# Routing of a two-layer streaming encoder on one core: the router's logits moved between the projection's products, and the first expert's tokens gathered by 10 wide products instead of 40 narrow ones

## The reference, cut to what matters

```python
def _moe(x, router_w, router_b, w_gate, w_up, w_down):
    xt = x.reshape(-1, D)
    logits = xt.astype(F32) @ router_w.astype(F32) + router_b.astype(F32)
    probs = jax.nn.softmax(logits, axis=-1)
    ...                      # best group, then top_p, top_i inside it -> combine
    for e in range(N_EXPERTS):
        h = jax.nn.silu(xt @ w_gate[e]) * (xt @ w_up[e])
        y = y + combine[:, e:e + 1] * (h @ w_down[e]).astype(F32)

# in each layer, after the mixer:
yp = _post_norm(yp, mp, ln_mix_g[l], ln_mix_b[l])
yp = _post_norm(yp, _moe(yp, router_w, router_b, moe_w_gate[l], moe_w_up[l], moe_w_down[l]), ln_ffn_g[l], ln_ffn_b[l])
```

## Time and profile before

| | |
|---|---|
| Median of three runs | 1509.43 us (1508.6 to 1513.21) |
| Profiled execution, own time | 1504.01 us |
| its span, first to last instruction | 1502.1 us |
| mean granted TensorE clock, share of full speed | 0.878 |
| PE busy | 1242.7 us (83%) |
| DVE busy | 1019.8 us (68%) |
| ACT busy | 701.2 us (47%) |

### The profile page before, as it was taken

The page is one execution under the profiler, slowest core; times in us unless marked ns, Lnnn a source line. Parts: engine busy times, 40 slices in busy tenths (PEclk is TensorE's granted clock), DMA queues, the critical chain, the costliest instruction groups (busy, mean ns, idle before and its releaser), DMA issues.

```text
span 1502.1 us, 17364 instructions
## 1 busy us (share of the span) xinstructions
PE 1242.7 (83%) x6836; PEld 995.0 (66%) x6836; DVE 1019.8 (68%) x1039; ACT 701.2 (47%) x623; POOL 199.3 (13%) x219
## 2 busy tenths in 40 slices
PE   6998998797889999996594362989978899999960
PEld 5898888585767766664473362967867676677740
DVE  5883656445468878786857998342464688888848
ACT  4642322104177777675123243541251777777730
POOL 2020000000400000001102972000004000000021
PEclk9998988697699999998796685999976999999985
DMA  9456010333589999997453008350135899999955
GB/s 271 192 60 115 5 60 6 83 127 112 192 319 391 385 378 385 371 379 272 104 83 72 0 3 64 113 198 13 45 112 193 318 380 379 376 388 387 388 163 154
DMA packets 79279, 301.79 MB, mean 201 GB/s; under 512 B 23156, under 2 KB 40912, under 8 KB 66864
## 3 DMA queue, kind: packets, MB, share of 16 engines
q1 hardware_dynamic: 63128, 246.07, 48.0%
q0 software_dynamic: 16096, 54.96, 11.7%
HBM read 265.01 MB, written 33.64 MB: 199 GB/s over the span
## 4 chain that ended last, share of the span: by engine, by line
PE 57%; DVE 20%; DMA 12%; ACT 5%; issue 4%; SPq 2%; POOL 0%; DVEq 0%; ACTq 0%; POOLq 0%
PE ps L2300 15%; PE ps L2302 14%; PE ps L2301 14%; DMA raw<-in_moe_w_down 7%; DVE wlo L695 4%; ACT whi L611 3%; PE ps L762 3%; DMA u_d<-ub 2%; PE ps L1706 2%; PE ps L378 2%; DVE s_jtmp L1508 1%; DMA raw<-in_w_in_ab 1%; PE ps L2410 1%; DVE s_wt L1465 1%; PE ps L1704 1%
## 5 line engine op out<-in xcount | busy, mean ns | idle before, releaser
L695 DVE TENSOR_TENSOR wlo<-raw,whi 128x4096 fp32r<-128x4096 f32 x92 | 406.6, 4421 | 124.8 <-ACT whi L611 124.8
L611 ACT ACTIVATE whi<-raw 128x4096 fp32r<-128x4096 f32 x92 | 333.7, 3629 | 121.2 <-DMA raw<-in_moe_w_down 108.1
L2300 PE MATMUL ps<-whi,xet_lo 128*96 128x512 f32 x528 | 213.5, 404 | 18.1 <-issue 13.6
L2302 PE MATMUL ps<-whi,xet_hi 128*96 128x512 f32 x528 | 210.6, 399 | 0.0
L2301 PE MATMUL ps<-wlo,xet_hi 128*96 128x512 f32 x528 | 210.3, 398 | 0.0
L2300 PEld LDWEIGHTS ps<-whi,xet_lo 128*96 128x96 f32 x528 | 88.0, 167 | 62.5 <-issue 28.7
L2300 PE MATMUL ps<-ft_hi,wlo 128*128 128x288 f32 x384 | 120.7, 314 | 5.9 <-DVE wlo L2047 3.4
L2301 PE MATMUL ps<-ft_lo,whi 128*128 128x288 f32 x384 | 117.7, 307 | 0.0
L2302 PE MATMUL ps<-ft_hi,whi 128*128 128x288 f32 x384 | 117.6, 306 | 0.0
L2302 PEld LDWEIGHTS ps<-whi,xet_hi 128*96 128x96 f32 x528 | 86.6, 164 | 37.5 <-issue 0.5
L2301 PEld LDWEIGHTS ps<-wlo,xet_hi 128*96 128x96 f32 x528 | 86.9, 165 | 33.5 <-issue 0.5
(11 more groups left out here) (453 smaller groups left out, 2225.5 us busy)
## 6 DMA issues: line engine op xcount, KB each, us to landing
raw<-in_moe_w_gate SPq DMA_DIRECT2D x32, 2048.0 KB, 9.9
raw<-in_moe_w_up SPq DMA_DIRECT2D x32, 2048.0 KB, 9.6
raw<-in_moe_w_down SPq DMA_DIRECT2D x32, 2048.0 KB, 10.1
yg<-ysb POOLq DMA_DIRECT2D x32, 384.0 KB, 6.0
xe<-xg POOLq DMA_DIRECT2D x30, 384.0 KB, 9.0
raw<-in_w_in_ab SPq DMA_DIRECT2D x16, 512.0 KB, 7.5
raw<-in_w_out_s SPq DMA_DIRECT2D x4, 2048.0 KB, 8.5
xg<-zeros POOLq DMA_DIRECT2D x4, 1536.0 KB, 14.8
```

Source lines behind the costliest of these rows:

```text
L611: sa.activation(whi[q][:], raw[q][:], ACT.Copy).then_inc(s(f"hi{q}" + L), 1)
L695: v.tensor_tensor(wlo[q][:], raw[q][:], whi[q][:].bitcast(F32), ALU.subtract).then_inc(s(f"lo{q}" + L), 1)
L2300: te.matmul(out, l_lo, r_hi, start=first, stop=False)
L2302: return te.matmul(out, l_hi, r_hi, start=False, stop=last)
```

## The change

It has three parts, each in both layers.

- The router's steps are issued one tile earlier or more. `route_between` puts a transpose (and once logits) between the two halves of a tile's projection, and `route_early` puts logits behind the tile. Only the last tile's transpose and logits stay in `route_pe`. ACT's copies and square roots are put in the matching order.
- `xt_first` holds `onehot` as the weights and moves `xtok` in rows of 512: 2 halves x 5 tiles, 10 products, into banks 2 and 3. The result is token-major, so ACT copies it half by half into `xe`, and PE transposes it with the 8 transposes that the other experts use (`x_turned`).
- `keep_warm` issues products whose result is not used (bank 2): four after the last logits, two after the counting products.

```diff
         def route_early(pe, l, i):
-            if i >= 3:
-                logits(pe, l, i - 3)
+            if i == 1:
+                x1_transpose(pe, l, 0)
             if i >= 2:
-                x1_transpose(pe, l, i - 2)
+                logits(pe, l, i - 1)
+
+        def route_between(pe, l, i):
+            if i == 2:
+                logits(pe, l, 0)
+            if i >= 2:
+                x1_transpose(pe, l, i - 1)
+
+        def keep_warm(x, n, bank, times):
+            for _ in range(times):
+                nc.tensor.matmul(ps[0:n, bank, :], ident[0:n, 0:n], x, start=True, stop=True)
 
         def route_pe(pe, l):
             te = nc.tensor
-            logits(pe, l, NT - 3)
-            x1_transpose(pe, l, NT - 2)
-            logits(pe, l, NT - 2)
             x1_transpose(pe, l, NT - 1)
             logits(pe, l, NT - 1)
+            keep_warm(xtok[0:TT, 0, 0:512], TT, 2, 4)
             pe.wait_ge(s("chosen"), 2 * l + 1)
...
                       ).then_inc(s("ranked"), 1)
+            keep_warm(xtok[0:TT, 0, 0:512], TT, 2, 2)
...
             hi(2, 0, "")
+            for half in range(2):
+                act.wait_ge(s("ranked"), 3 * l + 2 + half)
+                sa.activation(xe[0:CAP, 512 * half:512 * half + 512], ps[0:CAP, 2 + half, :], ACT.Copy).then_inc(s("r_exp"), 1)
             xt_hi(0)
...
                 pe.wait_ge(s("chosen"), 2 * l + 2)
-                for k in range(KT):
+                for half in range(2):
                     for i, (t0, n) in enumerate(TILES):
-                        ins = te.matmul(ps[:, 4 + k // 4, P * (k % 4):P * (k % 4) + CAP], xtok[0:n, i, k:D:KT],
-                                        onehot[0:n, i, :], start=(i == 0), stop=(i == NT - 1))
-                ins.then_inc(s("p_xt" + L), 1)
+                        ins = te.matmul(ps[0:CAP, 2 + half, :], onehot[0:n, i, :], xtok[0:n, i, 512 * half:512 * half + 512],
+                                        start=(i == 0), stop=(i == NT - 1))
+                    ins.then_inc(s("ranked"), 1)
+                pe.wait_ge(s("r_exp"), 3 * l + 3)
+                x_turned()
...
                     act.wait_ge(s("y"), 2 * NT + j + 1)
...
-                    if ph and i:
-                        ln_act(act, "mix1", [i - 1])
-                    if ph and i >= 2:
-                        x1t_copy(act, 1, i - 2)
+                    if ph and i == 1:
+                        x1t_copy(act, 1, 0)
+                    if ph:
+                        ln_act(act, "mix1", [i])
...
             for i in range(NT):
+                if i:
+                    x1t_copy(act, 0, i - 1)
                 ln_act(act, "mix0", [i])
-                if i >= 2:
-                    x1t_copy(act, 0, i - 2)
-            x1t_copy(act, 0, NT - 2)
             route_act(act, 0)
```

## The result

| | before | after |
|---|---|---|
| Median of 20 runs each, us | 1510.08 (1504.32 to 1515.80) | 1523.05 (1512.11 to 1533.23) |
| Ratio, 95% interval | | 1.0082 (1.0064 to 1.0099) |
| Profiled execution, own time | 1504.01 | 1522.25 |
| Span | 1502.1 | 1520.5 |
| Mean granted clock | 0.878 | 0.892 |

The change made the kernel slower by 0.8%; forecast was no change. The runs of one kernel differ by up to 21 us, and the medians of the kernel before by 8.6 from chip to chip (1501.5 to 1510.1). So the experiments are compared by their ratio to runs of the kernel before on the same chip. A profile shows one execution of them.

The account below looks back on a forecast made before the run. Two paths of some 30 us, over PE and over POOL and transfers, end together at the second expert's tokens. Terms -1.6 - 0.6 + 1.8 = -0.4 us gave 1503.6 profiled, 1509.0 on the median; range 1503 to 1515.

Parts of the forecast that it names:

- Logits inside the projection: Router: last product ends 4.9 us later, yet logits are read 2.0 us earlier in layer 0, 1.0 in layer 1.
- Ten wide products: Expert 0's gather: 8.65 us at full clock for 19.5; expert 0's first product 10.5 and 9.5 us earlier.
- The next wait: After expert 0's products, PE waits some 8 us for the second expert's tokens, where it did not wait before.
- I take the middle: Second expert's token load, layer 0: landing taken as 412.2, between 410.2 (undisturbed) and 414.1 (behind the third gate load).
- S: The second expert's first product, at 417.57 in layer 0; forecast at 415.95, 1.6 us earlier, and 0.6 earlier in layer 1.
- Rival 3: Second expert's token load waits for the whole 8.8 us gate load; +5.9 us, 1515.3; chance 0.12.
- Rival 1: Second expert's token load is not held up by the gate load; -4.4 us, 1505.0; chance 0.16.
- The clock at S: Products at S start at half clock after PE's wait; 0.9 us per layer counted against the gain.
- What moves S moves the end: Loop behind S: PE is nearly always busy (19.94 of 20 us), so a shift of S shifts the end.

Follow-up runs that it names:

- before_act: The kernel before with two one-column copies and two waits more on ACT in each layer, results unused; ratio 1.0041 (1.0018 to 1.0064).
- hold: The changed kernel, with the third gate matrix's load waiting until the second expert's tokens have landed; run twice, ratios 1.0021 and 1.0003 to the kernel before.
- half_products: The kernel before without every second block of expert 0's gather (20 products for 40), nothing added; ratio 1.0072 (1.0048 to 1.0096).
- hold_dve: The kernel hold with the two copies of expert 0's tokens made by DVE in place of ACT; ratio 0.9989 (0.9964 to 1.0013) to before.
- logits_only: The kernel before with only the logits and transposes issued inside the projection, the 40 products kept; run twice, ratios 0.9975 and 0.9985.

## Why the prediction was wrong, point by point

- **Logits inside the projection: right.** The last tile came 5.3 us later for 4.9, the logits were read 1.8 earlier for 2.0.
- **Ten wide products: right.** 8.83 us for 8.65 at full clock. Expert 0's first product came 10.4 earlier for 10.5.
- **The next wait: right in its place.** PE waited for the second expert's tokens, and the third gate load had caught up with their load.
- **The step that failed is "I take the middle".** I had the token load land between an undisturbed landing and one wholly behind the gate load, because "the lead here is half of that row's". How far the gate load is ahead does not matter: from 0 to 1.5 us, it takes the token load with it. Nor did the gate load take the 7.6 us that I used, but 9.2 to 9.8 where the two met. On the time axis of before, the tokens landed at 416.0 (423.1 less 7.1) for the 412.2 taken, and S at 419.5 for 415.95. In layer 1, counted from the logits, S came after 52.5 us for 50.6. Rival 3 had 415.3 and 419.05: it was the right case, and I gave it 0.12 against 0.65. Its reason for a slower gate load was wrong in layer 0, though: the last scatter had landed at 412.96, ahead of both issues, and the gate load was long because the token load shared the engines with it.
- **Rival 1 had the sharing wrong.** It took turns by packet to mean that the token load is not held up. The packets do take turns, but they are of 16 and of 4 KB, so sharing costs the small load nearly the whole time of the large one. The row at 450.40 does not speak against sharing: that load, issued behind the large one, sent its first packet 4.1 us after its issue, as the late ones here did.
- **The clock at S: undecided.** S began at half clock (0.71 us per product for 0.45), but over the 20 us from S in layer 0 the mean clock was 0.93 and 0.85 in the two profiles of after, for 0.91 in both of before.
- **"What moves S moves the end" holds in part.** It rests on PE being busy behind S. The DMA engines are as busy there (share 1.00), and the loop's time goes with the rate at which they move data, by several us from one execution to the next. The forecast had no term for it.
- **A term is missing.** Every number was counted from the start of the projection. That start moved. I counted nothing for stages whose instructions do not change; before_act shows 0.41% from two small copies and two waits per layer on ACT alone.

Two profiles of each kernel, their means and differences in us, show where the 12.4 went:

| Piece | before | after | difference |
|---|---|---|---|
| to the start of layer 0's projection | 287.5 | 292.4 | +4.8 |
| to the reading of the logits | 78.8 | 77.0 | -1.9 |
| to S | 50.4 | 54.2 | +3.8 |
| loop behind S | 278.6 | 280.4 | +1.8 |
| to the reading of layer 1's logits | 424.3 | 423.3 | -1.1 |
| to S of layer 1 | 50.1 | 52.7 | +2.6 |
| loop behind it | 277.0 | 279.6 | +2.6 |
| to the end of the span | 56.5 | 56.2 | -0.3 |

The two rows "to S" are the collision, shown by hold and half_products. The first row is put down to ACT's longer program by before_act and hold_dve; its size is rough, since the two profiles of after are 6.4 us apart in it (295.6 and 289.2). That ACT's program acts through the moment at which instructions are loaded is argued from the q14 rows, not shown. The rows of the loops are within the scatter. The parts by themselves, half_products' 0.72%, before_act's 0.41% and logits_only's -0.15 to -0.25%, make 0.9 to 1.0%, for the 0.8% of the whole; each has an interval of 0.2% or more to either side.

Open: in the two profiles of hold, S stands 7.5 us earlier than in before in sum (logits to S 47.4 and 47.3 us in the mean, for 50.4 and 50.1, and 1.7 more ahead of it in layer 0), less 2.9 us by which the projection starts later. That leaves some 4.6 us that the ratios of 1.0003 and 1.0021 do not show. The loops scatter by that much, and the two profiled executions of hold are 14.2 and 3.1 us under the medians of their runs, so they may not stand for them. No run isolates it.

## What to carry to other kernels

When a change makes one of two paths shorter that end together, look for the transfers that the shorter path also releases: one that is issued earlier may now stand ahead of the small load on which the other path ends. Look at the size of the packets as well: turns of one packet each favour the load with the larger ones. A small load on the critical path needs its own moment: one wait on the large load that follows it gave back some 9 us here. And an edit can cost time in a stage that it does not touch, so compare the milestones of the whole program, over several profiles, before a difference is put down to the stage that was edited.

## What the runs showed of the hardware

- **A small load beside a large one.** The token load, 384 KB, took 3.4 to 3.8 us alone and 8.1 to 9.8 with the 2 MB gate load issued from 1.5 us ahead to 0.3 behind; a lead of 1.09 us freed it, and the gate load then took 11.5. The Trainium skill (DMA: Bandwidth & Descriptors, section on queues, rings and completion order) says that a DMA engine takes turns between queues, a packet at a time. The trace agrees where the token load had begun: 67 packets of each load from 407 to 411 us in half_products. But turns are equal in packets and not in bytes, 16 KB to 4 KB here, so the small load took 8.6 to 8.8 us and not twice its time alone. The rule leaves open why a token load issued level or behind sent its first packet only after 3.8 to 4.5 us, for 1.3.
- **Waiting for code.** With two copies and two waits more per layer on ACT, PE waited 5.6 us for nothing that the profile shows, for 1.9 to 3.2 in the six profiles without copies on ACT, about 250 us ahead of the added work. That is in or next to a stretch of small transfers: the DMA share from 112 to 120 us was 1.3 to 1.9 (a sum over packets, which may pass 1) at only 24 to 33 GB/s, in the profiles with the long wait and without it. The Trainium skill (Runtime: NRT & Kernel Launch, section on instruction fetch mechanics) says that engines refill their instruction memory in 16 KiB blocks over a DMA queue of their own, and that the cost is mostly hidden. PE's 5.6 us here are not hidden. That they come from such a refill among small transfers is argued and not shown.
